# Moving work across the stage borders of a two-layer diffusion block with experts

## The reference: what is computed

```python
h, hc = layer_norm(x, ...), layer_norm(ctx, ...)
for l in range(2):
    u, uc = h * (1 + sc1) + sh1, hc * (1 + csc1) + csh1
    y, y_ctx = token_mixer(u, uc, w_in[l], ...)      # conv + attention + mLSTM, gated, one projection
    h = layer_norm(alpha * h + g1 * y, ...)          # context likewise, in layer one only
    u2 = h * (1 + sc2) + sh2
    f = grouped_moe(tokens, w_router, b_router, moe_w_gu[l], moe_w_dn[l])
    h = layer_norm(alpha * h + g2 * f, ...)          # context likewise, in layer one only
return h
```

## Time and profile before

| what | value |
|---|---|
| runs | 1885.26, 1889.02, 1914.2 us |
| median | 1889.02 us |
| profiled execution | 1886.55 us |
| its span | 1884.8 us |
| mean granted TensorE clock | 0.946 |

### The profile page before, as it was taken

The page is one execution under the profiler, slowest core; times in us unless marked ns, Lnnn a source line. Parts: engine busy times, 40 slices in busy tenths (PEclk is TensorE's granted clock), DMA queues, the critical chain, the costliest instruction groups (busy, mean ns, idle before and its releaser), DMA issues.

```text
span 1884.8 us, 30599 instructions
## 1 busy us (share of the span) xinstructions
PE 1664.2 (88%) x12508; PEld 1002.6 (53%) x12508; DVE 832.9 (44%) x1724; ACT 375.8 (20%) x904; POOL 194.3 (10%) x227
## 2 busy tenths in 40 slices
PE   4999999999999999789999864999999994988852
PEld 1454466554444458544555433767678884544421
DVE  3079426665101012653225536592761116554554
ACT  2001035532000010322222111013731001221200
POOL 0300000000000000022333230000000000323211
PEclk9999999999999999789999986999999996999976
DMA  9623544630321232489569994332004545799993
GB/s 309 169 68 112 201 171 165 224 101 26 100 67 51 83 112 67 187 337 402 200 246 397 406 338 142 107 117 79 23 1 139 188 157 206 308 408 409 406 406 116
DMA packets 188829, 365.11 MB, mean 194 GB/s; under 512 B 23285, under 2 KB 107773, under 8 KB 187923
## 3 DMA queue, kind: packets, MB, share of 16 engines
q1 hardware_dynamic: 176784, 331.48, 49.0%
q0 software_dynamic: 10704, 25.16, 3.8%
q10 hardware_dynamic: 1203, 6.51, 1.0%
HBM read 356.79 MB, written 14.42 MB: 197 GB/s over the span
## 4 chain that ended last, share of the span: by engine, by line
PE 59%; issue 19%; DVE 7%; POOL 6%; DMA 6%; ACT 2%; SPq 1%; POOLq 0%; DVEq 0%; ACTq 0%
PE psum L803 56%; POOL ys L757 4%; DMA yab<-in_moe_w_gu 3%; POOL qkT L747 2%; SPq L648 1%; PE psum L987 1%; DMA arena<-ys 1%; DMA convT<-us,x_row 1%; DMA ring<-in_w_mod 1%; DVE arena L1832 1%; POOL convT L727 0%; PE psum L865 0%; ACT uT L1311 0%; DMA ys<-qkT,y_row 0%; DVE H L2069 0%
## 5 line engine op out<-in xcount | busy, mean ns | idle before, releaser
L803 PE MATMUL psum<-uT,ring 128*128 128x512 f32 (+1 forms) x1472 | 504.8, 503 | 4.0 <-ACT uT L1311 4.0
L803 PEld LDWEIGHTS psum<-uT,ring 128*128 128x128 f32 x1472 | 280.7, 191 | 223.1 <-issue 204.5
L803 PE MATMUL psum<-ring,mo_tok 128*32 128x256 f32 x4992 | 323.7, 393 | 47.8 <-DVE ring L2058 44.6
L803 PEld LDWEIGHTS psum<-ring,mo_tok 128*32 128x32 f32 x4992 | 149.2, 111 | 176.8 <-DVE ring L2058 76.4
L803 PE MATMUL psum<-ring,v_tok 128*32 128x256 f32 x2496 | 156.9, 390 | 5.0 <-DVE ring L2058 4.2
L2058 DVE COPY ring<-yab 128x1024 f32<-128x1024 f32 x120 | 86.6, 746 | 153.2 <-PE psum L803 109.9
L1702 DVE SCALAR_TENSOR_TENSOR convT<-upad,cwT,convT 128x512 f32<-128x512 f32 (+1 forms) x240 | 132.4, 614 | 2.1
L1897 DVE TENSOR_TENSOR arena<-psum,mqk 128x512 f32<-128x512 f32 (+1 forms) x16 | 8.9, 557 | 254.6 <-PE psum L803 254.6
L2058 DVE COPY ring<-arena 128x1024 f32<-128x1024 f32 x120 | 82.2, 706 | 79.0 <-DMA arena<-in_moe_w_dn 50.1
L803 PEld LDWEIGHTS psum<-ring,v_tok 128*32 128x32 f32 x2496 | 80.4, 113 | 66.6 <-issue 10.4
L803 PE MATMUL psum<-ring,uT 128*128 128x256 f32 (+1 forms) x576 | 113.7, 357 | 0.0
(11 more groups left out here) (288 smaller groups left out, 1594.2 us busy)
## 6 DMA issues: line engine op xcount, KB each, us to landing
yab<-in_moe_w_gu SPq DMA_DIRECT2D x120, 512.0 KB, 14.8
uT<-in_moe_w_gu SPq DMA_DIRECT2D x120, 512.0 KB, 14.8
arena<-in_moe_w_dn SPq DMA_DIRECT2D x120, 512.0 KB
ring<-in_w_in SPq DMA_DIRECT2D x104, 512.0 KB, 4.7
ring<-in_w_mod SPq DMA_DIRECT2D x96, 512.0 KB, 5.7
ring<-in_w_out SPq DMA_DIRECT2D x16, 512.0 KB, 4.4
ring<-in_moe_w_gu SPq DMA_DIRECT2D x16, 512.0 KB, 5.5
ring<-in_w_a_out SPq DMA_DIRECT2D x8, 512.0 KB, 3.6
```

Of the source, the lines that this page charges most:

```text
L803: return nc.tensor.matmul(dst, lhsT, rhs, start=start, stop=stop)
```

## The change

It does seven things.

1. **Layer two's start.** PE transposes the latent half, makes `val` and `gate` of the first slot, and only then transposes the context half. ACT's order follows.
2. **Layer one's norm before the experts.** `nat` of the first half is no longer made between the two halves: tile 0 is turned back after the second half's transposes, tiles 1 to 3 after `scores`. The second half's copies to `uT` are shared by ACT and DVE, not all on DVE. ACT takes the second square root after the first half's copies, not in their middle.
3. **ACT's tables.** A one-column Sigmoid ahead of the router rows and a one-column Silu ahead of the first quad's copy, both into `table_row`.
4. **Loads held back.** SP waits for the gathers of tiles 0 and 1 before layer two's first weights; POOL waits for all gathers before the norm's rows (and so the `wgate` loads behind them); in layer one SP waits for the first quad's gather before it stages expert 1.
5. **The last norm** is done by tile: statistics right after each tile's sums; subtract mean and multiply by gain in one operation, scale and add bias in another.
6. **The output** leaves by tile, in two DMAs of 512 KB.
7. `upad` is cleared only in its margins.

```diff
 def on_scalar(which, h, k, tiles):
-    if tiles == 2:
-        return k % 2 == 1
-    return h == 0 or (which == 0 and k == KD // 2 - 1)
+    if which:
+        return k % 2 == 1 or (tiles > 2 and h == 0)
+    return h == 0 or k == KD // 2 - 1
...
             def load_when_free(key):
                 n = index[key]
+                if key == ("a", 1, 0):
+                    for t in range(2):
+                        sp.wait_ge(gathered[t], 16)
...
                         elif x == 0:
                             wait_ready(sp, "yb", l, KD - 1)
+                            if l == 0:
+                                sp.wait_ge(quad_loaded[0], 16)
...
-            sp.wait_ge(h_ready, sum(NORM_TILES))
-            sp.dma_start(out.rearrange("b (t p) d -> p (b t) d", p=P), H[:, 0:2, :]).then_inc(out_sent, 16)
-            sp.wait_ge(out_sent, 16)
+            for t in range(2):
+                sp.wait_ge(h_ready, sum(NORM_TILES) - 1 + t)
+                sp.dma_start(out[0, t * P:(t + 1) * P, :], H[:, t, :]).then_inc(out_sent, 16)
+            sp.wait_ge(out_sent, 32)
...
                 pool.wait_ge(up_ready, blk_base[l] + nb)
+                for t in range(nt):
+                    pool.wait_ge(gathered[t], 16 * (l + 1))
                 load_norm_rows(2 * l + 2)
...
                     by_channel(w, 0, n, "val", l, j)
                     by_channel(w, P, n, "gate", l, j)
+                    if l and j == 0:
+                        transposes(0, 1)
+                if l:
+                    inputs_ready(1)
...
                 for h in range(nt // 2):
                     transposes(1, h)
+                    if h:
+                        natural(0)
...
                         if which:
-                            after_first(h)
+                            if h == 0:
+                                if tiles > 2:
+                                    norm_std(w, 1)
+                                f(table_row[:, :], eps[:, :], ACT.Sigmoid)
+                            else:
+                                natural(0)
+                            wait_ready(act, "router", l, h)
...
                 act.wait_ge(routed, 2 * l + 1)
                 act.wait_ge(rows_used, 2 * l + 2)
+                f(table_row[:, :], eps[:, :], ACT.Silu)
                 quad_copy(0, 0)
...
-                link(v.memset(upad[:, :, :, :], 0.0))
+                v.memset(upad[:, :, :, 0:PAD], 0.0)
+                link(v.memset(upad[:, :, :, PAD + S_LAT:], 0.0))
...
+            for t in range(2):
+                add_experts(t)
+                statistics(t).then_inc(ln_var, 1)
+            dve.wait_ge(ln_loaded, 32 * (2 * DEPTH + 1))
+            for t in range(2):
+                dve.wait_ge(ln_var, norm_halves(2 * DEPTH) + t + 1)
+                link(v.scalar_tensor_tensor(H[:, t, :], H[:, t, :], mv[:, t, 0:1], ln_g, ALU.subtract, ALU.mult))
+                dve.wait_ge(ln_std, norm_halves(2 * DEPTH) + t + 1)
+                link(v.reciprocal(rstd[:, t:t + 1], sd[:, t:t + 1]))
+                v.scalar_tensor_tensor(H[:, t, :], H[:, t, :], rstd[:, t:t + 1], ln_b, ALU.mult, ALU.add).then_inc(h_ready, 1)
```

## The result

| | before | after |
|---|---|---|
| runs, us | 1885.26, 1889.02, 1914.2, 1920.56 | 1855.12, 1857.39, 1854.94, 1857.3 |
| median, us | 1901.61 | 1856.21 |
| profiled execution, us | 1886.55 | 1855.12 |
| its span, us | 1884.8 | 1853.3 |
| mean granted clock | 0.946 | 0.957 |

The ratio of the times is **0.9844**, 95% interval 0.9831 to 0.9857: the change takes some 29 us off, between 27 and 32. It leaves out the two executions of before over 1900 us, which are disturbed, so it goes by 1885 to 1889 and not by that median. Measured a second time (experiment 9), the same kernel stood at 0.9864 (0.9844 to 0.9883), 26 us. The forecast was 1859 within 1851 to 1868; the median is 1856.21.

A forecast was written before the change was run, and what follows sets the result against it. PE was taken to bound the kernel, except at layer ends, where it waits on store, gather and norms. Terms 4.0 + 6.9 + 11.1 + 0.2 + 3.0 + 1.5 + 1.1 = 27.8 off 1886.55 gave 1859, range 1851 to 1868.

The forecast's parts named there:

- what a measurement can tell: Whole kernel: a measurement tells about 2%, 38 us, from no change; faster 0.10, within 2% 0.88, slower 0.02.
- no listed rival but one, with 0.03: Border to layer two: held weights arrive too late and make the kernel slower than before, 1887 or more; chance 0.03.
- Store to gather: Layer one's end: with the weights waiting, the last store to `ys` lands sooner, 2.9 us back.
- The last gather: Layer two's end: without the norm's rows beside it the gather goes from 8.17 to 5.2, 3.0 us (0 to 4.2).
- the last norm and output: The kernel's end: norm by tile gains 1.5 us, the half-sized last output DMA 1.1.
- the rival that they swallow it: Layer one's experts: their DMA-full stretches swallow the 4.0 us gained ahead of them, giving 1863; chance 0.05.
- the reordering: Layer two's start: first pair hidden, copy wait gone, transposes at a better clock; 11.1 us (8.7 to 11.7).
- the rival that the clock stays down: Border to layer two: the whole first pair runs at 1.2 GHz, takes 13.8 us, giving 1865; chance 0.12.
- the gather: Layer one's end: without small-piece weights beside it the first gather goes from 9.21 to 5.2 us, 4.0 back.
- The rival that gathers don't gain: Both layer ends: a gather is paced by its own reads of `ys`, so 4.0 and 3.0 vanish, 1866; chance 0.15.
- layer one's norm: Norm and routing before layer one's experts: `scores` 4.8 us earlier, of which 3.5 are left at `count` (2.0 to 5.8).
- the table: Layer one's first expert block: the Silu table's load, 1.28 us, no longer stands before the first Silu; 1.3 us gained.

The follow-up runs named there:

- experiment 9: The changed kernel, unaltered, measured a second time; its profile is the one called "again"; median 1858.42 us, ratio 0.9864.
- experiment 1: The changed kernel, but SP sends layer two's first weights without waiting for the gathers of tiles 0 and 1; 1863.87 us, ratio 0.9891.
- experiment 8: The changed kernel, but the last norm takes both tiles in one and the output leaves in one DMA, as before; 1859.74 us, ratio 0.9873.
- experiment 6: The changed kernel, but the one-column Silu stands ahead of ACT's waits for the routing and rows_used; 1853.57 us, ratio 0.9841.
- experiment 2: The changed kernel, but POOL loads the norm's rows and the `wgate` loads behind them without waiting for the gathers; 1862.59 us, ratio 0.9885.
- experiment 3: The changed kernel, but POOL loads the norm's rows at once and only the `wgate` loads wait for the gathers; 1860.86 us, ratio 0.9868.
- experiment 5: The changed kernel, but layer one's norm has its old order of `nat`, copies and square root; tables stay; 1862.41 us, ratio 0.9884.
- experiment 11: The changed kernel without the one-column Silu, so the table loads just before the first real Silu; 1852.68 us, ratio 0.9834.
- experiment 10: The changed kernel with the one-column Silu ahead of ACT's two waits, measured again; 1854.55 us, ratio 0.9848.
- experiment 4: The changed kernel, but at layer two's start PE transposes both halves before the first products, as before; 1867.15 us, ratio 0.9908.
- experiment 7: The changed kernel, but SP stages expert 1 in layer one without waiting for the first quad; 1856.36 us, ratio 0.9853.

## Why the prediction was right, and where it failed

**The step that failed** is the one on what a measurement can tell: "about 2%, 38 us, from no change", for which the prediction gives no row. The four runs after lie within 2.5 us, and the ratio's interval reaches 0.0013 to either side, some 2.5 us; from the first measurement to the second the ratio moved by 0.0020, 3.8 us. The forecast gain of 27.8 was seven times that. I put 0.88 on no difference beside a sum that no listed rival but one, with 0.03, brought to nothing. By its own working it should have said faster. The time itself lay 2.8 above what came.

**Right in mechanism and size.** Store to gather, 3.1 for 2.9 (experiment 1 undoes exactly it). The last gather 3.4 for 3.0; the last norm and output 3.2 for 2.6 (experiment 8: 3.1 in place); the quad's hold nothing; layer two's experts, paced by DMA, took nothing from the moved table. The order at layer one's experts gave its gain on, apart from 0.35: the rival that they swallow it fell.

**Right in mechanism, lucky in size: the reordering.** It gave 11.2 for 11.1, and 10.9 came back in the median when it was undone. But 11.2 rests on a first pair at 1.00, which took 7.1. In experiments 6 and 9 it took 10.1, and there the reordering is worth 8.5 against the one profile of before, just under the 8.7 that I had as the lower bound. So the rival that the clock stays down, with 13.8 for the pair, came in part, in some executions and not in others. Layer two's norm and routing, 0.74 for 0.2, is such luck too: it took 37.2 to 37.4 in all the other profiles, 0.1 to 0.3 less than before.

**Right in size, wrong in cause: the gather.** I had 4.0 from SP's weights in small pieces; it was 4.36. But experiments 1 to 3 show that POOL's loads alone, rows and gate columns, bring back all of it, and SP's weights alone 2.05. The rival that gathers don't gain fell too. By the Trainium skill (DMA: Bandwidth & Descriptors, Queues, rings and completion order) the later gathers of ACT's queue would not slow the first: here it takes 4.97 with three behind it and 4.92 with one, so the trace agrees. It did not come down to the 4.0 of that estimate, though, and that the estimate's 1856.5 is the measured time is chance.

**Mis-sized: layer one's norm.** `scores` gained 4.4 for 4.8. Then I had 1.8 more for eight more `nat`, at 0.23 each, and took 1.3 of it off. But all 24 ran at full clock, 2.82 / 24 = 0.12 each, and `g2` at 3.74, not 4.48, so `count` gained 5.9 for 3.5 and now waits for DVE instead of PE. The granted clock was 0.50 to 0.52 from 771 to 777 before, and 1.00 from 764 to 774 after. That PE now stands still less ahead of this stretch is the likely reason, and only argued; experiment 5 has both the old order and the old 3.65 us. The term came out 2.4 us above the forecast at `count`, 2.6 at the first product.

**Mis-sized the other way: the table.** "The load that stood before the first Silu is gone" was worth 1.3 in the sum, because the Silu followed its load at once. First product to first Silu took 7.69 before and 7.70 after. In the first place, the Silu also waits for the first block's last `up` product, and the load ran beside these products. The timeline of before, cut at that product, which is the last of the 24:

```profile
816.29 1.50 PE L803 MATMUL psum<-ring,mo_tok 128*32 128x256 f32 x24
```

That product ended at 817.79 and the Silu started at 818.36, 0.57 behind it; after, it starts 0.07 behind the same product. So the load held the Silu for 0.5 us, not 1.28; with the load back in that place (experiment 11) it is 0.5 again. In the second place, from the first product to this one PE took 7.12 us before and 7.63 after, by its clock, and that is the 0.5. I had left both out of this term. Against either other place of the load the new one costs 2.0 to 2.5 at the first Silu (experiments 6, 10, 11). The drain of 1.38 that the Trainium skill (ScalarE: Activation LUTs, What ACT_TABLE_LOAD costs) adds does not show: the one-column Silu starts 0.01 us after the load ends.

By the table of stages these two are +2.6 and -1.7 (0.35 lost where 1.3 was forecast); the other rows add 1.4, so it is 30.1 for 27.8, and the clock's accidents add 1.3 in the profiled pair. In the profile "again" the two are +2.6 and -1.5, the reordering -2.6 and the others +1.0, in all 27.3. That this is so near to 27.8 is luck: errors of both signs cancel.

## What to carry to other kernels

Before calling a gain "no difference", compare its sum with the interval that repeated measurements give, not with a round figure. Where a DMA ends the critical chain, hold back all that would run beside it, small-piece loads and broadcast rows first, and let the next engine's work start with whichever half is ready. A table load belongs in idle time of its engine. Ahead of an operation that PE waits for it cost about its own length, 1.25 us of 1.28, and there it was worse than where it had stood. Before counting such a load as a gain, look when the next operation's other input is ready: here that left 0.5 of 1.28. And take a second profile before calling a stage's gain exact: here one stage differed by 2.7 us between two executions of the same kernel.

## What the runs showed of the hardware

- **One and the same code costs some 3 us more or less by the clock.** The stretch from 464 to 470 behind a PE wait of 2.85 us was granted 0.50 before and 1.00 after; in experiments 3 to 9 it was 1.00, in 1, 2, 10 and 11 0.72. The context of layer one was normed at 754.9 to 755.5 in those at 1.00, at 757.3 to 758.4 in the others; the four at 0.72 had another such stretch, 0.66 from 372 to 377. The runs of experiments 10 and 11 fall in two groups, 1851.4 to 1854.6 and 1856.9 to 1859.4; what parts them is not shown. The Trainium skill (TensorE: Matmul & The Clock Gate, What's actually happening) says that how much of a kernel's start runs at the lower clock varies from run to run; here it does so in mid-kernel.
- **The same waits do not bring the same clock.** At the border to layer two PE stood still for 21.3 us, made 16 transposes and waited 1.65 us more, in the change as in experiment 9. The first pair then ran at 1.00 in the one and at 0.70 in the other, 7.14 us against 10.09.
- **Neighbours of a gather do not add up.** 1 MB from `ys` took 4.97 us with only its own queue behind it, 7.02 beside SP's weights, 7.47 beside the norm's rows, 9.61 beside rows and 16-byte pieces, and 9.33 beside all of them.
